# First projection's weight stored block by block, projection steps placed between the attentions' first scores, and squares added by Pool in the scan: one Trainium2 core

## The reference

```python
h = rms_norm(x, norm_w)
proj = h @ w_in                     # cut into qkv_dn, z_dn, b_dn, a_dn, qkv_att, gate_att
y_dn = deltanet_branch(qkv_dn, z_dn, b_dn, a_dn, ...)     # o = rms_norm(scan) * silu(z)
y_att = dilated_attention_branch(qkv_att, gate_att, ...)
x = x + concatenate([y_dn, y_att]) @ w_out
```

## Time and profile before

| what | value |
|---|---|
| time before, median of 3 runs | 1130.64 us (1129.4 to 1132.56) |
| time of the profiled execution | 1136.13 us |
| its span, first to last instruction | 1134.3 us |
| PE busy / DVE / ACT / POOL | 1101.9 / 632.4 / 471.3 / 485.5 us |
| granted TensorE clock, mean | 0.990 |

### The profile page before, as it was taken

One profiled execution on the slowest core, in us unless ns is written; L12 is line 12 of the kernel. 1 busy time (PEld: TensorE's weight loads), 2 busy tenths in 40 slices (PEclk: granted clock), 3 DMA queues, 4 the chain that ended last, 5 costly groups with the idle time before them and its releaser, 6 DMA issues.

```text
span 1134.3 us, 16005 instructions
## 1 busy us (share of the span) xinstructions
PE 1101.9 (97%) x5909; PEld 878.3 (77%) x5909; DVE 632.4 (56%) x1253; ACT 471.3 (42%) x806; POOL 485.5 (43%) x376
## 2 busy tenths in 40 slices
PE   6999999999999999999999999999999999999997
PEld 5778777777787877777777778878888888888886
DVE  4256888767745685887758856487433434310003
ACT  5246344465654445544335455444332232312124
POOL 4534233355252453333323315444544545444352
PEclk9999999999999999999999999999999999999999
DMA  8759675510330434444312103532333342332311
GB/s 172 158 107 205 121 139 121 135 45 1 123 104 7 127 104 129 124 146 147 121 60 75 61 20 107 167 94 75 111 110 97 88 111 76 109 111 75 111 37 75
DMA packets 114802, 116.36 MB, mean 103 GB/s; under 512 B 4817, under 2 KB 97191, under 8 KB 114740
## 3 DMA queue, kind: packets, MB, share of 16 engines
q1 hardware_dynamic: 99952, 88.68, 30.1%
q10 hardware_dynamic: 14212, 26.13, 7.2%
q0 software_dynamic: 576, 0.73, 0.2%
HBM read 113.41 MB, written 2.12 MB: 102 GB/s over the span
## 4 chain that ended last, share of the span: by engine, by line
PE 93%; DVE 2%; DMA 2%; ACT 1%; issue 1%; SPq 0%; POOL 0%; DVEq 0%; ACTq 0%
PE bank L694 26%; PE bank L696 25%; PE bank L695 25%; PE bank L915 3%; PE bank L889 2%; PE bank L896 2%; DMA raw<-w_in 2%; PE bank L988 1%; PE bank L1072 1%; PE bank L1057 1%; PE bank L837 1%; PE bank L731 0%; PE bank L1099 0%; PE bank L1101 0%; PE bank L886 0%
## 5 line engine op out<-in xcount | busy, mean ns | idle before, releaser
L491 POOL TENSOR_TENSOR wlo<-raw,whi 128x512 fp32r<-128x512 f32 x312 | 423.4, 1388 | 570.9 <-ACT whi L1318 570.9
L694 PE MATMUL bank<-h_hi,whi 128*128 128x512 f32 x952 | 383.6, 403 | 6.3 <-POOL wlo L491 3.5
L695 PE MATMUL bank<-h_lo,whi 128*128 128x512 f32 x952 | 372.7, 392 | 0.0
L696 PE MATMUL bank<-h_hi,wlo 128*128 128x512 f32 x952 | 372.7, 391 | 0.0
L694 PEld LDWEIGHTS bank<-h_hi,whi 128*128 128x128 f32 x952 | 180.1, 189 | 58.5 <-issue 15.3
L1318 ACT ACTIVATE whi<-raw 128x2048 fp32r<-128x2048 f32 (+1 forms) x79 | 150.2, 1902 | 172.3 <-PE bank L696 154.6
L696 PEld LDWEIGHTS bank<-h_hi,wlo 128*128 128x128 f32 x952 | 179.8, 189 | 38.7
L695 PEld LDWEIGHTS bank<-h_lo,whi 128*128 128x128 f32 x952 | 180.3, 189 | 36.0 <-issue 1.5
L1447 ACT ACTIVATE pT_a<-bank 128x256 f32<-128x256 f32 (+3 forms) x80 | 32.4, 406 | 176.7 <-PE bank L896 176.3
L1859 DVE SCALAR_TENSOR_TENSOR ada_acc<-ada_w,small,ada_acc 128x512 f32<-128x512 f32 x84 | 72.6, 865 | 3.1 <-DMA ada_w<-w_ada 2.3
L2304 DVE SCALAR_TENSOR_TENSOR x_res<-bank,modc,x_res 128x512 f32<-128x512 f32 x8 | 6.0, 750 | 114.1 <-PE bank L696 114.1
(11 more groups left out here) (377 smaller groups left out, 1523.9 us busy)
## 6 DMA issues: line engine op xcount, KB each, us to landing
raw<-w_in SPq DMA_DIRECT2D x66, 512.0 KB, 5.8
ada_w<-w_ada ACTq DMA_DIRECT2D x96, 256.0 KB, 3.0
raw<-w_up SPq DMA_DIRECT2D x44, 512.0 KB, 4.7
raw<-w_down SPq DMA_DIRECT2D x22, 512.0 KB, 4.1
raw<-w_out SPq DMA_DIRECT2D x16, 512.0 KB, 4.6
x_tok<-x SPq DMA_DIRECT2D x4, 512.0 KB, 5.9
toe<-bias_rows SPq DMA_DIRECT2D x8, 256.0 KB, 13.7
raw<-w_branch_swa SPq DMA_DIRECT2D x4, 512.0 KB, 3.5
```

Of the source, the lines that this page charges most:

```text
L491: pool.tensor_tensor(wlo[s][:, c], raw[s][:, c], whi[s][:, c].bitcast(F32), ALU.subtract)\
L694: pe.matmul(ps, wh, h_hi, start=start, stop=False)
L695: pe.matmul(ps, wh, h_lo, start=False, stop=False)
L696: return pe.matmul(ps, wl, h_hi, start=False, stop=stop)
```

## The change

1. **Weight layout.** The host program hands `w_in` over cut into the 17 blocks (`in_blocks`), each partition's 8 x 256 numbers of a block side by side, where they were 8 pieces of 1 KB from rows of 16,416 bytes. Each half of a block is now one piece of 4 KB per partition (2 KB for block 0). SP no longer waits for block 0 to land before it issues block 1. ACT makes `hi(0)` behind the first `h_hi`, no longer ahead of it.
2. **Steps between first scores.** `attention` calls `between(k)` after the scores of the first maps. In `a1` two of the eight steps that stood ahead of the first scores move there, in `a2` one of four (and two of the other three move behind the transposes of v), in `a3` four of eight, two behind each pair. ACT reads the tile that these steps end (`gate_tiles(..., -1)`) in the tail of unit 0 for `a1` and `a3`, no longer ahead of the attention. In `a3` the steps per unit go from 6 to 5.5, so that unit 15 has six where it had none. One step of the delta rule's preparation moves from unit 10 to unit 11 of `norm_steps`.
3. **Behind the third attention** ACT makes `hi(N_S3 + 1)` ahead of the last norm and the first pair of sigmoids ahead of the last `h_hi`.
4. **Scan.** ACT scales `qsq` by EPS x 128 x 128 when it copies it; POOL adds it onto `Dk` for the first three chunks (`add_squares`), and `out_sum` needs one product for them, two only for the last. `out_sum(c)` moves one chunk later on PE, and ACT's `rsqrt` with it.

```diff
+def in_blocks(w):
+    w = w[0].reshape(KT, P, D_IN)
+    return np.concatenate([w[:, :, o:o + (P if n == 0 else 256)].transpose(1, 0, 2).reshape(P, -1)
+                           for n, o in enumerate(OFFS)], 1)
...
             for n in range(17):
-                if n == 0:
-                    weights(n, cols(w_in, OFFS[n], P))
-                    sp.wait_ge(S["raw_full0"], 32)
-                else:
-                    weights(n, cols(w_in, OFFS[n]))
+                weights(n, in_block(n))
...
+            def add_squares(c):
+                pool.wait_ge(S["dn_osq"], c + 1)
+                pool.tensor_tensor(Dk[c % 2][:, :, :], Dk[c % 2][:, :, :], qsq[:, :, c * P:(c + 1) * P], ALU.add).then_inc(S["dn_diag"], 1)
+            add_squares(0)
+            add_squares(1)
             for e in range(TT - 1):
+                if e == 0:
+                    add_squares(2)
...
-        norm_steps = lambda w: 137 + w if w < 8 else 144 + 3 * (w - 7) + w // 12
+        norm_steps = lambda w: 137 + w if w < 8 else 144 + 3 * (w - 7) + w // 12 - (w == 10)
-        diff_steps = lambda w: min(136 + 6 * (w + 1), 28 * KT)
+        diff_steps = lambda w: min(136 + 11 * (w + 1) // 2, 28 * KT)
...
                 for g in range(2 * M):
+                    if g == 2:
+                        between(0)
                     qk(g)
+                between(M - 1)
...
-                pe.matmul(bank[2 + c % 2][:, :], m(C_EPSQ), qsq[:, :, c * P:(c + 1) * P], start=True, stop=False)
-                pe.wait_ge(S["dn_osq"], c + 1)
+                if last:
+                    pe.matmul(bank[2 + c % 2][:, :], m(C_INVH), qsq[:, :, c * P:(c + 1) * P], start=True, stop=False)
+                    pe.wait_ge(S["dn_osq"], c + 1)
+                else:
+                    pe.wait_ge(S["dn_diag"], 8 + c + 1)
                 pe.matmul(bank[2 + c % 2][:, :], m(C_INVH), Dk[c % 2][:, :, :].rearrange("p h i -> p (h i)"),
-                          start=False, stop=True).then_inc(S["dn_osum"], 1)
+                          start=not last, stop=True).then_inc(S["dn_osum"], 1)
...
-                    out_sum(c - 1)
+                    if c >= 2:
+                        out_sum(c - 2)
...
-            hi(0)
             for kt in range(KT):
+                if kt == 1:
+                    hi(0)
                 act.wait_ge(S["xn_done"], kt + 1)
...
-            gate_tiles(dil_steps, -1)
...
             def tail1(w):
+                if w == 0:
+                    gate_tiles(dil_steps, -1)
                 gate_tiles(dil_steps, w)
```

More of the change, by code:

```diff
@@ L382, in cols, with in_block @@
                 return dsts
+            def in_block(n):
+                c, size = (BLK * n - BLK // 2, BLK // 2) if n else (0, BLK // 4)
+                return lambda r: [(r[:, h * size:(h + 1) * size], a["w_in"][:, c + h * size:c + (h + 1) * size]) for h in range(2)]
             sp.dma_start(mats[:, C_ID, :], a["k_mats"][:, 0:P]).then_inc(S["x_in_ident"], 16)
@@ L813, in _ @@
                     pe.wait_ge(S["cols_ready"], 2)
-                gemm(n, tiles_of(n)[0], (0,) if n == 0 else (0, 1), ready=(S["rms_lo"], before("n0", "lo") + 1) if n == 0 else None)
+                if n == 0:
+                    gemm(n, 0, (0,), stride=P, ready=(S["rms_lo"], before("n0", "lo") + 1))
+                else:
+                    gemm(n, tiles_of(n)[0])
                 if n == 0:
@@ L866, in unit_fold, with attention @@
                     fold(p0 // 8 + w // 8 - 1)
-            def attention(tag, units, tail=None):
+            def attention(tag, units, tail, between):
                 units = list(units)
@@ L937, in attention @@
                     tail(len(units))
-            attention("a1", units_a1(), dilated_fill)
+            attention("a1", units_a1(), dilated_fill, lambda k: gate_steps(dil_steps, -1, slice(6, 8)))
             def key_sum(h):
@@ L1175, in swa_fill @@
                 unit_fold(ADA_A2, w)
-            attention("a2", units_a2(), swa_fill)
+            attention("a2", units_a2(), swa_fill, lambda k: gate_steps(swa_steps, -1, slice(3, 4)))
             for t in range(8, 12):
@@ L1196, in d_sum @@
                 pe.matmul(bank[OB["a3"][h % 2]][:, :], m(C_INVH), osq[:, :], start=True, stop=True).then_inc(S["d_sum"], 1)
[L1198 removed]
+            attention("a3", units_a3(), diff_norm, lambda k: gate_steps(diff_steps, -1, slice(4 + 2 * k, 6 + 2 * k)))
             evac(pe, T_S3 - 2)
@@ L1508, in _ @@
             act.wait_ge(S["tile_ready"], 33)
-            act.activation(qsq[:, :, :], qsq0[:, :, :], ACT.Copy).then_inc(S["dn_egc"], 1)
+            act.activation(qsq[:, :, :], qsq0[:, :, :], ACT.Copy, scale=EPS * P * P).then_inc(S["dn_egc"], 1)
             for l in range(N_LVL - 1):
@@ L1533, in _ @@
                 act.activation(kbe[:, c], four(bank[UW[c % 2][1]][:, :]), ACT.Copy).then_inc(S["dn_w"], 1)
-            for c in range(TT + 2):
+            for c in range(TT + 3):
+                if 2 <= c < TT + 2:
+                    e = c - 2
+                    act.wait_ge(S["dn_osum"], e + 1)
+                    if e >= 2:
+                        act.wait_ge(S["dn_scaled"], e - 1)
+                    rsqrt(four(bank[2 + e % 2][:, :]), ktail[:, 2 * (e % 2)], ktail[:, 2 * (e % 2) + 1], "dn_ors", eps_q)
                 if c < TT:
@@ L1540, in _ @@
                     act.activation(Dk[c % 2][:, :, :], four(bank[SCAN_OUT[c]][:, :]), ACT.Square).then_inc(S["dn_osq"], 1)
[L1541 to L1549 removed]
+                if c >= 3:
+                    e = c - 3
                     act.wait_ge(*((S["dn_mix"], e + 1) if e < TT - 1 else (S["dn_mix_last"], 1)))
@@ L1644, in diff_tail, with gate_pair @@
                     act.activation(osq[:, :], of[h % 2][:, :], ACT.Square).then_inc(S["d_sq"], 1)
-            gate_tiles(diff_steps, -1)
+            def gate_pair(q):
+                pair = sg[:, :, :].rearrange("p (g q) t -> p g q t", g=2)[:, :, q, :]
+                act.activation(pair, pair, ACT.Sigmoid).then_inc(S["sig_ready"], 1)
             attention("a3", units_a3(), diff_tail)
             diff_hi(2)
+            hi(N_S3 + 1)
             d_norm(3)
+            gate_pair(0)
             diff_hi(3)
-            hi(N_S3 + 1)
             for j in range(4):
@@ L1655, in _ @@
                     hi(N_S3 + j + 1)
-                for q in (2 * j, 2 * j + 1):
-                    pair = sg[:, :, :].rearrange("p (g q) t -> p g q t", g=2)[:, :, q, :]
-                    act.activation(pair, pair, ACT.Sigmoid).then_inc(S["sig_ready"], 1)
+                for q in ((2 * j, 2 * j + 1) if j else (1,)):
+                    gate_pair(q)
                 for q in (2 * j, 2 * j + 1):
```

36 lines of the change are left out of this document (16 added, 20 removed).

## The result

| what | before | with the change |
|---|---|---|
| median of 6 runs | 1131.82 us (1129.4 to 1135.98) | 1123.87 us (1122.98 to 1125.15) |
| ratio, 95% interval | | 0.9924 [0.9909, 0.9938] |
| time of the profiled execution | 1136.13 us | 1123.83 us |
| its span, its mean granted clock | 1134.3 us, 0.990 | 1122.0 us, 0.995 |

The change makes the kernel 8 us faster. The two profiled executions are 12.3 us apart, though, as forecast. The question is why two executions show what the medians do not.

A forecast was written before the change was run, and what follows sets the result against it. PE bounds the kernel, busy 1101.9 of 1134.3 us; gains come from its waits, work and half-clock stretches. Seven terms, 4.3 - 1.4 + 1.0 + 2.1 + 1.0 + 1.7 + 4.0 = 12.7, give 1117.9 us; range 1114 to 1122.8.

The forecast's parts named there:

- the clock terms: Half-clock stretches on PE expected to go: 1.7 us at the start, others at the third attention's begin and end.
- the sum's last line: End of the forecast: the median lies 5.5 us below the profiled execution, same subtracted; 1130.64 - 12.7 = 1117.9 us.
- third attention's begin: First scores after four steps, new 1.9 us wait for DVE's copies of v; gain 1.7 us if clock holds.
- the clock falls at one of the new waits: Rival: clock drops at the wait ahead of block 0 or at the third attention; price 1.7, 1119.6 us, chance 0.20.
- Third attention's end: Six steps fill unit 15, removing PE's waits for ACT and slow products; sigmoids' wait goes too; gain 4.0 us, bounds 0.5-4.4.
- by a hair: Behind the third attention: hi(N_S3 + 1) holds the last norm 1 us longer, which branch products just cover.
- The start: Block 1 loads right behind block 0; its products start 2.6 us earlier at full clock, 1.7 more; gain 4.3 us.
- rate as before, only the SP wait saved: Lower bound at the start: block 1's load no faster, result -0.5 us.
- the layout gives nothing: Rival at the start: block 1 lands as late as before, loss 0.5 instead of gain 4.3; 1122.7 us, chance 0.08.
- First attention: At its begin, ACT's moved tap delays DVE's taps, so PE waits 1.3 us more at unit 1; loss 1.4 us.
- preparation: Moved delta-rule step removes PE's 1.41 us wait for DVE, meets ACT's copy, about half a us; gain 1.0 us.
- scan: Three products of 0.86 us go, new waits at chunk 1 and last sum, last h_lo wait goes; gain 2.1 us.

## Why the prediction was wrong

**What bounds the kernel, and the mechanisms: right.** Each forecast wait stood in the profile after, at its place and within 0.3 us, and the sum over the stages met the difference of the two profiles (12.3 for 12.7). That meeting is in part luck: two stretches that I had not priced (behind the row norm and where the scan begins) gave 3.3, the longer one behind the first attention took 1.7 back, and the wait of 1.65 that I missed took the rest.

**The failed step: the clock terms, and the sum's last line.** "The median of the runs is 5.5 below that execution, and I subtract the same from it." That treated the 5.5 as a constant of the profiling. Against the mean of 61 later runs, 1132.9, the execution was 3.2 long, and 2.8 of that was the clock: at 0.990 it lost 11.4 us to half-clock stretches, where those runs lost 8.6 on average and the changed kernel's 6.2. The other 2.3 of the 5.5 is that my base was short: the three runs with the median of 1130.64 lay under the mean, at a time that the 61 runs have at a clock of 0.994 or 0.995. And three terms of my sum (1.7 at the start, 1.7 in the third attention's begin, 2.0 at its end) were such stretches. The same microseconds were in the surplus of 5.5 and in the gain. At full clock the sum was 12.7 - 5.4 = 7.3, and the runs show 5.8; of the clock's 5.4 they show 2.4. That is 8.2 in all. So the 6.0 us between 1117.9 and 1123.9 are 3.0 of clock, 1.5 at full clock and 2.3 of base, less 0.8 by which the median of the result lies under the mean of all 13 runs of the changed kernel.

The stretches fall at fixed places, but at most of them in some executions only. Over 14 profiles:

| place | at half clock in |
|---|---|
| behind the wait for block 1 | 1 of 2 with that wait, 0 of 12 without |
| behind the row norm's wait of 1.06 | 4 of 14 |
| behind the first attention | 14 of 14, 7 us long in 5, 3.4 in 9 |
| where the scan begins | 7 of 14, 7 us long in 3 |
| third attention's begin | 8 of 14 |
| end of the third attention, without steps | 1 of 4 |
| the same with six steps | 0 of 10 |
| last tile | 14 of 14 |

So a stretch in one profile is worth its 1.7 us only times the share of executions that have it. By the counts above the three stretches of my sum are worth 0.9 + 0.4 + 0.4 = 1.7, an estimate from few profiles, where I had 5.4. The stretch at the third attention's end, priced at 2.0 where one of 3.4 us can lose 1.7, was in one profile of four; that at the begin came in three of the four kernels with no steps between the pairs, and in five of ten with steps. The rival "the clock falls at one of the new waits" (1119.6) was closer than the forecast, but for another reason: behind the new wait of 1.65 it fell sometimes, as it had behind the old ones.

**Third attention's end: a wait missed, 1.65 us.** I wrote that the branch products cover ACT's delay "by a hair". I counted ACT's 1 us and not what ACT's instruction releases: POOL's split. I had the row for that (1.62 instead of 0.62 in the scan) and looked for it in the scan alone. 7.3 - 1.65 is 5.7, beside the 5.8 of the runs; as undoing the move gave the runs 0.6 to 1.1 back and not 1.65, so close a match is partly chance. The part's own sum is loose as well: its terms are 3.0 and 1.3, which is 4.3, and no term makes it 4.0.

**The start: right in size, wrong in reason.** 2.6 without clock, 2.2 to 2.5 measured. I took the load's rate to decide, and gave "rate as before, only the SP wait saved" a loss of 0.5. Measured, dropping SP's wait alone saved all of it but 0.4 +- 0.3. I hadn't worked out when a slow block 1, issued at once, would land: 1.5 MB at the 126 GB/s of its window are 12 us from 10 on by my estimate, and ACT comes at 22.5 in that kernel. The rival "the layout gives nothing" was right on the layout and wrong on what follows: its 1122.7 is the number nearest to the median, by luck, for the start did gain.

**First attention, preparation, scan, second attention: right.** -1.4 (a loss of 0.7 to 1.8 in three comparisons), 1.0 (0.6 between the profiles with the clock's 1.7 out: a wait of 1.58 went and one of 0.75 for ACT's copy came, which would leave 0.8), 2.1 (1.8), 1.0 (1.3).

## What to carry to other kernels

When the profiled execution is slower than the median, find out first what makes it so, and take it off the terms that are of the same kind before anything is added up; multiply a run's time by its granted clock to compare kernels at a third of the scatter (0.65 us for 1.9 over the 61 runs). When a step is moved on one engine, follow what it releases on the others: ACT's instruction took 1.9 us where it stood and held the norm for 0.6, and POOL's answer to it cost DVE 1.9. Before a transfer is made faster, ask when its consumer comes, and whether it was merely issued late.

## What the runs showed of the hardware

**The granted clock.** Every stretch at half clock inside the program was 3.4 us or 7 us long, at places where PE had waited or had run short products (behind the first attention, in all 14 profiles, 32 products of one column that took 3.7 to 5.0 us); the kernel before had six of them in one execution and two in another. 1.07 us of time go with each 0.001 of the mean clock.

**Loads from rows.** In the same two windows of the start, pieces of 1 KB from rows of 16,416 bytes came at 119 and 84 GB/s with the DMA engines 1.04 and 0.98 busy; from rows of 17,408 bytes with each piece at a multiple of 1,024 they came at 278 and 372 with 1.14 and 1.06. The Trainium skill lets transfers from 512 bytes on run at line rate (DMA: Bandwidth & Descriptors, Specifications); here the aligned pieces bear it out (372 GB/s, beside 399 for pieces of 4 KB) and the others don't. The Trainium skill also says (DMA: Bandwidth & Descriptors, How a descriptor splits into AXI transactions) that a descriptor that starts off a 256-byte boundary costs one transaction more, so five for 1 KB in place of four. By that, an estimate from this count of the Trainium skill, the rate would fall by a fifth at most; it fell to 43% and 23%, so more than that is at work, and no run here tells what.
